# Two transformer blocks on one core: the first weights loaded in two halves, and the parameter rows moved behind them, in the lead-in of the kernel

## The reference, cut to what matters

```python
for i in range(DEPTH):
    h = rmsnorm(x, ln1_g[i]) @ w_in[i]
    (fq, fk, fv, ff, dq, dk, dv, c_q, c_kv, k_r) = jnp.split(h, split_points, axis=-1)
    o_fox = fox_group(fq, fk, fv, ff, fgate_b[i])
    o_diff = diff_group(dq, dk, dv, lam_q1[i], lam_k1[i], lam_q2[i], lam_k2[i], diff_norm_g[i], lam_init)
    o_mla = mla_group(c_q, c_kv, k_r, q_norm_g[i], w_uq[i], kv_norm_g[i], w_ukv[i], pos)
    x = x + jnp.concatenate([o_fox, o_diff, o_mla], axis=-1) @ w_o[i]
    up = causal_dwconv(rmsnorm(x, ln2_g[i]) @ w_up[i], conv_w[i], conv_b[i])
    g, u = up[..., :D_FF], up[..., D_FF:]
    x = x + (jax.nn.silu(g) * u) @ w_down[i]
x = rmsnorm(x, final_g)
...
```

## Time and profile before

| | |
|---|---|
| time, median of 3 runs | 1857.57 us (1857.36 to 1857.59) |
| span of the profiled execution, first to last instruction | 1854.4 us |
| the time outside that span (launch and end), by the median | 3.2 us |
| PE busy | 1454.0 us (78%) |
| DVE busy | 799.2 us (43%) |
| ACT busy | 571.2 us (31%) |
| moved by DMA | 563.14 MB, mean 304 GB/s |

### The profile page before, as it was taken

The page is one execution under the profiler, slowest core; times in us unless marked ns, Lnnn a source line. Parts: engine busy times, 40 slices in busy tenths (PEclk is TensorE's granted clock), DMA queues, the critical chain, the costliest instruction groups (busy, mean ns, idle before and its releaser), DMA issues.

```text
span 1854.4 us, 24842 instructions
## 1 busy us (share of the span) xinstructions
PE 1454.0 (78%) x10541; PEld 1069.3 (58%) x10541; DVE 799.2 (43%) x1246; ACT 571.2 (31%) x898; POOL 62.2 (3%) x56
## 2 busy tenths in 40 slices
PE   8999999999999999985555445579999555555546
PEld 7999999989999898861212112149886121111212
DVE  5767777776777799830101001019973010000101
ACT  4655555465554585321000000028532100000001
POOL 1010000010000000100000000002010000000000
PEclk9999999999999999998777778789999877777868
DMA  9426555534655385799999999997479999999997
GB/s 325 145 70 226 191 174 173 171 104 154 199 182 182 110 271 161 294 372 430 429 430 430 430 429 429 430 394 245 153 293 369 430 429 429 430 430 429 430 429 315
DMA packets 165492, 563.14 MB, mean 304 GB/s; under 512 B 12600, under 2 KB 116534, under 8 KB 137606
## 3 DMA queue, kind: packets, MB, share of 16 engines
q1 hardware_dynamic: 155318, 551.49, 76.2%
q10 hardware_dynamic: 10064, 10.06, 1.8%
HBM read 558.05 MB, written 1.05 MB: 301 GB/s over the span
## 4 chain that ended last, share of the span: by engine, by line
PE 54%; issue 23%; DMA 17%; DVE 3%; ACT 2%; POOL 1%; SPq 0%; POOLq 0%; PEldq 0%; ACTq 0%; DVEq 0%
PE psum L2682 6%; PE psum L2721 5%; PE psum L2976 5%; PE psum L2659 5%; PE psum L2661 5%; PE psum L2660 5%; DMA ring<-in_w_down 5%; DMA ring<-in_w_up 3%; DMA arena<-in_w_gate 3%; PE psum L2711 3%; PE psum L2831 2%; PE psum L2958 2%; PE psum L2576 2%; DMA arena<-in_w_down 2%; DMA arena<-in_w_up 2%
## 5 line engine op out<-in xcount | busy, mean ns | idle before, releaser
L2976 PE MATMUL psum<-ring,arena 128*32 128x512 f32 (+1 forms) x1600 | 280.6, 691 | 198.4 <-DMA ring<-in_w_down 77.8
L2976 PE MATMUL psum<-arena 128*32 128x512 f32 x1024 | 207.6, 702 | 149.5 <-DMA ring<-in_w_up 40.3
L2976 PEld LDWEIGHTS psum<-ring,arena 128*32 128x32 f32 x1600 | 70.7, 128 | 346.0 <-issue 343.4
L907 DVE TENSOR_TENSOR W<-ring,W 128x2048 fp32r<-128x2048 f32 (+1 forms) x92 | 206.3, 2243 | 85.1 <-ACT W L888 84.5
L2274 DVE TENSOR_TENSOR arena<-arena,psum 128x512 f32<-128x512 f32 x16 | 11.0, 690 | 452.7 <-PE psum L2976 452.7
L2659 PE MATMUL psum<-XT,W 128*128 128x256 f32 x704 | 199.4, 283 | 0.0
L2661 PE MATMUL psum<-XT,W 128*128 128x256 f32 x704 | 199.1, 283 | 0.0
L2660 PE MATMUL psum<-XT,W 128*128 128x256 f32 x704 | 199.0, 283 | 0.0
L888 ACT ACTIVATE W<-ring 128x2048 fp32r<-128x2048 f32 (+1 forms) x92 | 172.3, 1872 | 78.7 <-PE psum L2661 42.5
L2976 PEld LDWEIGHTS psum<-arena 128*32 128x32 f32 x1024 | 50.5, 127 | 251.4 <-issue 251.4
L2660 PEld LDWEIGHTS psum<-XT,W 128*128 128x128 f32 x704 | 134.9, 192 | 0.9
(11 more groups left out here) (341 smaller groups left out, 2619.0 us busy)
## 6 DMA issues: line engine op xcount, KB each, us to landing
ring<-in_w_down SPq DMA_DIRECT2D x36, 2048.0 KB, 30.0
ring<-in_w_up SPq DMA_DIRECT2D x32, 2048.0 KB, 31.2
ring<-in_w_up SPq DMA_DIRECT2D x58, 1024.0 KB, 5.1
ring<-in_w_gate SPq DMA_DIRECT2D x28, 2048.0 KB, 33.5
ring<-in_w_in SPq DMA_DIRECT2D x54, 1024.0 KB, 7.6
arena<-in_w_up SPq DMA_DIRECT2D x24, 2048.0 KB, 32.9
arena<-in_w_down SPq DMA_DIRECT2D x20, 2048.0 KB, 29.9
arena<-in_w_gate SPq DMA_DIRECT2D x20, 2048.0 KB, 29.8
```

What stands on the lines that cost most here:

```text
L907: nc.vector.tensor_tensor(W2[split_pair(v)][:, c], slot(v % SLOTS_1)[:, c], W1[split_pair(v)][:, c].bitcast(F32), ALU.subtract).then_inc(r ...
L2976: last = nc.tensor.matmul(psum[CAP * e:CAP * (e + 1), b, 0:cols.stop - cols.start], src[:, 4 * half + k, CAP * e:CAP * (e + 1)], tiles[e][ ...
```

## The change: what it does

1. SP loads block 0 in two halves, `k` 0 and 1, then `k` 2 and 3; the six parameter rows of SP come only after block 1 and piece 2.
2. ACT makes the first parts of `k` 2 and 3 first, then rounds the first half of block 0, the second half, and makes the first parts of `k` 4 to 7. Only then does it issue its seven parameter rows and `wf`, and goes on to block 1.
3. DVE makes the second parts of `k` 0 to 3 before the difference of block 0; its four copies of turned parameter rows come after the copy of the norm's root.
4. PE starts `latents(0)` when the first half is rounded, without the transposes of parameter rows; in it the products with `XT2` go ahead of those with `W2`. The four transposes come after the two of the norm's root, into bank 7 in place of 6, and the wait for the copies moves from block 2 to block 3.

```diff
@@ sync
-                        sp.dma_start(raw_latents(i), columns(w["w_in"], lay, c0, n)[:, 4 * i:4 * i + 4]).then_inc(slot_loaded[i], 16)
                         if lay == i == 0:
+                            src = columns(w["w_in"], lay, c0, n)
+                            sp.dma_start(raw_latents(i)[:, 0:2], src[:, 0:2]).then_inc(s_lamr, 16)
+                            sp.dma_start(raw_latents(i)[:, 2:4], src[:, 2:4]).then_inc(slot_loaded[i], 16)
+                        else:
+                            sp.dma_start(raw_latents(i), columns(w["w_in"], lay, c0, n)[:, 4 * i:4 * i + 4]).then_inc(slot_loaded[i], 16)
+                    else:
+                        load(u % SLOTS_1, columns(w["w_in"], lay, c0, n), n)
+                        if lay == 0 and i == 2:
                             sp.wait_ge(s_zero, 5)
                             for dst, src in parameter_rows()[1::2]:
                                 sp.dma_start(dst, src).then_inc(s_rows, 16)
-                    else:
-                        load(u % SLOTS_1, columns(w["w_in"], lay, c0, n), n)
@@ scalar
-            for dst, src in parameter_rows()[0::2]:
-                act.dma_start(dst, src).then_inc(s_rows, 16)
-            act.dma_start(wf, w["w_in"][0].rearrange("(k p) n -> p k n", p=P)[:, :, 768:772]).then_inc(wu_loaded, 16)
             act.wait_ge(s_small, SMALL)
...
-                    split_round(act, past, 0)
-                if lay == 0:
                     act.wait_ge(s_gain, 18)
-                turn_split_act(act, past, 0, 0, par[:, C_LN1:C_LN1 + 8] if lay else first_gain_cols, FIRST_BANK[lay], ENTRY_BY_DVE[lay])
-                if lay == 0:
+                    turn_split_act(act, past, 0, 0, first_gain_cols, FIRST_BANK[lay], ENTRY_BY_DVE[lay] + tuple(range(4, KD)))
+                    act.wait_ge(s_lamr, 16)
+                    nc.scalar.activation(latent_weights(W1[0])[:, 0:2], raw_latents(0)[:, 0:2], ACT.Copy).then_inc(s_lame, 1)
+                    act.wait_ge(slot_loaded[0], 16)
+                    act.sem_clear(slot_loaded[0])
+                    nc.scalar.activation(latent_weights(W1[0])[:, 2:4], raw_latents(0)[:, 2:4], ACT.Copy).then_inc(rounded, 1)
+                    turn_split_act(act, past, 0, 0, first_gain_cols, FIRST_BANK[lay], tuple(range(4)))
+                    for dst, src in parameter_rows()[0::2]:
+                        act.dma_start(dst, src).then_inc(s_rows, 16)
+                    act.dma_start(wf, w["w_in"][0].rearrange("(k p) n -> p k n", p=P)[:, :, 768:772]).then_inc(wu_loaded, 16)
                     split_round(act, past, 1)
@@ vector
-                    if k == 2 and lay == 0:
+                    if k == 4 and lay == 0:
+                        dve.wait_ge(s_lame, 1)
                         split_rest(dve, past, 0)
-                        parameters()
...
                 nc.vector.tensor_copy(root_cols, psum[:, 1, 0:S]).then_inc(root_table, 1)
+                if lay == 0:
+                    parameters()
@@ tensor
-            pe.wait_ge(s_rows, ROWS)
-            for l in range(DEPTH):
-                for i in range(2):
-                    nc.tensor.transpose(psum[:, 6, P * (2 * l + i):P * (2 * l + i + 1)], rows[:, l, i, :], ident).then_inc(s_rowsT, 1)
...
-                    pe.wait_ge(rounded, past(rounded) + SPLIT_AT[i] + 1)
+                    if lay == i == 0:
+                        pe.wait_ge(s_lame, 1)
+                    else:
+                        pe.wait_ge(rounded, past(rounded) + SPLIT_AT[i] + 1)
                     for k in range(4 * i, 4 * i + 4):
+                        if lay == i == 0 and k == 2:
+                            pe.wait_ge(rounded, past(rounded) + SPLIT_AT[i] + 1)
...
+                    if lay or i:
+                        with_rests()
                     for k in range(4 * i, 4 * i + 4):
                         pe.wait_ge(xt_rest, past(xt_rest) + k + 1)
...
+                    if lay == i == 0:
+                        with_rests()
...
                 last.then_inc(root_table, 1)
+                if lay == 0:
+                    pe.wait_ge(s_rows, ROWS)
+                    for l in range(DEPTH):
+                        for i in range(2):
+                            nc.tensor.transpose(psum[:, 7, P * (2 * l + i):P * (2 * l + i + 1)], rows[:, l, i, :], ident).then_inc(s_rowsT, 1)
```

More of the change, by code:

```diff
@@ L534, in build @@
         s_lamd = sem("lambda_dots_differences_and_ones")
-        s_lame = sem("setup_exps")
+        s_lame = sem("first_half_rounded_then_setup_exps")
         slot_loaded = [sem(f"slot_loaded{i}") for i in range(SLOTS)]
@@ L546, in quad_loaded @@
             return slot_loaded[ring_slot(lay, 2 + q % QUAD_SEMS)]
-        s_lamr = sem("lambda_rows")
+        s_lamr = sem("first_half_loaded_then_lambda_rows")
         wu_loaded = sem("mla_weights_loaded")
@@ L683, in before @@
             return past
-        SMALL, ROWS, LAMBDA_ROWS = 16 * 2, 16 * 13, 16 * 5
+        SMALL, ROWS, LAMBDA_ROWS = 16 * 2, 16 * 13, 16 + 16 * 5
         def parameter_rows():
@@ L1176, in _ @@
                     act.dma_start(wf, w["w_in"][lay].rearrange("(k p) n -> p k n", p=P)[:, :, 768:772]).then_inc(wu_loaded, 16)
+                    turn_split_act(act, past, 0, 0, par[:, C_LN1:C_LN1 + 8], FIRST_BANK[lay], ENTRY_BY_DVE[lay])
                 else:
-                    split_round(act, past, 0)
-                if lay == 0:
                     act.wait_ge(s_gain, 18)
-                turn_split_act(act, past, 0, 0, par[:, C_LN1:C_LN1 + 8] if lay else first_gain_cols, FIRST_BANK[lay], ENTRY_BY_DVE[lay])
-                if lay == 0:
+                    turn_split_act(act, past, 0, 0, first_gain_cols, FIRST_BANK[lay], ENTRY_BY_DVE[lay] + tuple(range(4, KD)))
[8 more added lines that the diff above has]
+                    act.dma_start(wf, w["w_in"][0].rearrange("(k p) n -> p k n", p=P)[:, :, 768:772]).then_inc(wu_loaded, 16)
                     split_round(act, past, 1)
@@ L1603, in parameters @@
                         dve.wait_ge(s_rowsT, 2 * DEPTH)
-                        nc.vector.tensor_copy(par_all[:, l, P * i:P * i + P], psum[:, 6, P * (2 * l + i):P * (2 * l + i + 1)]).then_inc(s_par, 1)
+                        nc.vector.tensor_copy(par_all[:, l, P * i:P * i + P], psum[:, 7, P * (2 * l + i):P * (2 * l + i + 1)]).then_inc(s_par, 1)
                 dve.wait_ge(s_par, 2 * DEPTH)
@@ L1621, in lambdas @@
                     if l == 0:
-                        dve.wait_ge(s_lame, 1)
+                        dve.wait_ge(s_lame, 2)
                     nc.vector.tensor_tensor(par_all[:, l, C_NLAM:C_NLAM + 1], lame[:, 2 * l + 1:2 * l + 2],
@@ L1648, in lower_bounds @@
                 step(nc.vector.tensor_tensor(lb_t[:, 12:16], low[1], lb_t[:, 0:4], ALU.subtract))
-                dve.wait_ge(s_lame, 2)
+                dve.wait_ge(s_lame, 3)
                 step(nc.vector.tensor_tensor(lb_t[:, 16:20], lb_t[:, 8:12], lb_t[:, 12:16], ALU.add))
@@ L2393, in latents, with with_rests @@
                                              start=(k == 0), stop=False)
-                    split_ready(i)
-                    for k in range(4 * i, 4 * i + 4):
-                        for t in range(TT):
-                            nc.tensor.matmul(banks[t], XT1[:, k, t * P:(t + 1) * P], w2[:, k % 4, 0:LATENTS],
-                                             start=False, stop=False)
+                    def with_rests():
+                        split_ready(i)
+                        for k in range(4 * i, 4 * i + 4):
+                            for t in range(TT):
+                                nc.tensor.matmul(banks[t], XT1[:, k, t * P:(t + 1) * P], w2[:, k % 4, 0:LATENTS],
+                                                 start=False, stop=False)
+                    if lay or i:
+                        with_rests()
                     for k in range(4 * i, 4 * i + 4):
@@ L2420, in block @@
                         split_ready(i)
-                        if lay == 0 and i == 2:
+                        if lay == 0 and i == 3:
                             pe.wait_ge(s_par, 2 * DEPTH)
```

## The result

The changed kernel takes 1864.89 us (median of 5 runs, 1863.72 to 1866.15) beside 1857.57 us of the kernel before (5 runs, 1856.0 to 1858.9). The ratio is 1.0041, with a 95% interval of 1.0031 to 1.0052: 7.3 us slower, and the interval leaves out 1. The forecast was 1865.3 us.

What follows compares the result with a forecast made beforehand. PE bounds the first 18 of 40 slices, then DMA; lead-in shifts of PE reach the end one for one. 5.4 + 1.9 + 0.4 = 7.7 us takes 1857.57 to 1865.3 us, range 1862.7 to 1868.6 (chance 0.62).

Steps and rivals of the forecast that it cites:

- First products at 10.2: Lead-in, PE: first products start at 10.2 us, behind its last transpose, in place of 12.2.
- the clock gives most of that back: First 24 products: with the clock still rising at 14.9 us they end at 16.5, 1.0 us earlier; otherwise 14.4.
- `wf` issued at 13.6: ACT's eight issues begin at 10.2 us; `wf`, the last, follows 3.37 us later, at 13.6.
- Travel 8.4: `wf` takes 8.4 us from issue to landing, at 22.0 us; 5.8 and 9.4 kept as bounds.
- Narrow products +5.4: PE waits for `wf`: narrow products start at 22.9 us, not 17.54, +5.4 us (+2.8 to +6.4).
- Clock 1.9: Behind PE's idle wait, 3.8 us of work at half speed lose 1.9 us (0 to 4.2).
- Transposes 0.4: Four parameter-row transposes, turned later, add 0.4 us to PE; their DVE copies cost nothing.
- 3.2 us outside the span: Whole kernel: the median lies 3.2 us above the span, so span 1862.1 us gives median 1865.3.
- as meant: Rival: `wf` lands in time, by 15.6 us, 2.0 us after issue; 1857.0 us, at best 1854.9; chance 0.16.
- Short wait: Rival: ACT's queue gets its turn beside SP's backlog, `wf` lands after 5.8 us; 1860.8 to 1862.7 us; chance 0.19.
- Longer: Rival: `wf` finds SP's queue deeper, or the clock comes back late twice; over 1868.6 us; chance 0.03.
- The halves don't come sooner: Rival: SP delivers block 0's first half only at 9.9 us, first products start at 11; forecast time unchanged.

Runs made afterwards that it cites:

- gate first: Changed kernel with `wf` issued early, and its rounding on ACT and difference on DVE put ahead of block 1's: 1856.09 us, ratio 0.9992.
- 68 idle products: Changed kernel with 68 idle products in front of PE's wait for the rounded gate columns: 1870.58 us, ratio 1.0076.
- keeping PE busy: Changed kernel with 34 idle products in front of PE's wait for the rounded gate columns: 1862.82 us, ratio 1.0031.
- `wf` early: Changed kernel with `wf` issued where it stood before, behind ACT's table load, the seven parameter rows staying late: 1856.23 us, ratio 0.9996.

## Why the prediction was right, point by point

- **What bounds it.** "Every microsecond by which PE's products move" goes to the end: shown. PE lagged 7.40 us at block 2 and 7.42 at 407 us. For the changed kernel and all ten variants, the shift of block 2 in the profile and the difference of the medians agree within 1.3 us, from -2.1 and -0.9 (gate first) to +12.5 and +13.4 (68 idle products).
- **First products at 10.2:** 9.89. ACT's two first parts took 0.84 us, as estimated, but started at 8.21. The gain of the change was there, and hidden. The step "the clock gives most of that back", with a rise still at 14.9, was wrong: the clock rose within the first eight products, so the 24 ended at 14.45, near the lower of the two figures given (14.4 and 16.5). The whole 3.1 us went into a longer wait, and so this error did not touch the sum.
- **`wf` issued at 13.6:** 12.93. ACT's eight issues start at 9.84, and the last begins 3.09 us after the first, not 3.37.
- **Travel 8.4:** the reading was an upper bound, since the next issue of ACT at 13.42 only shows that `wf` had landed by then, and no packet of the queue moved after 12.6. It measured 8.6 to the activation (the chain's piece is 8.61), 8.3 and 9.3 in the two runs that issued it elsewhere. The choice of "the same transfer beside the same load" over the 256-packet row was the right one.
- **Narrow products +5.4:** +4.7 (22.23 against 17.54). The 0.7 us over are those of the issue time; a travel 0.2 us longer and hand-overs 0.2 us shorter than allowed (21.56 to 22.23, 0.7 in place of 0.9) cancel. This is the term that was over-priced.
- **Clock 1.9:** the granted clock was 0.50 for 4.87 us, and keeping PE busy gave back 2.3. Under-priced by 0.4 in this execution, over-priced by 0.6 in another of the same lead-in (1.3); both inside 0 to 4.2.
- **Transposes 0.4:** the six take 0.58 us (31.48 to 32.06) against 0.13 for two before, so 0.4. The copies of DVE at nothing: PE has no wait at blocks 2 or 3.
- **Sum 7.7 in the lead-in:** 7.4. The 0.7 us too much for `wf` and the 0.4 too little for the clock offset each other, and of the agreement to 0.4 us that much is luck; in an execution with the cheaper clock the lead-in's lag was 6.35.
- **3.2 us outside the span:** wrong. It is 1.8. The prediction took the difference between one profiled execution and the median of others for a part outside the span. This did not matter, since the sum was added to the median. It does explain why the spans differ by 9.0 us and the medians by 7.3: the profile of the kernel before is of an execution some 1.4 us faster than its median, one of the two that kept the clock at 400 us (1.2 us).
- **Range of the forecast:** its lower end, 1862.7, doesn't follow from the reason given. The sum without any of the clock's price is 1863.4 us.

Of the rivals, "as meant" fails by its own criterion: `wf` would have had to travel 2.0 us, less still with the 24 products ending at 14.45, and even with SP's queue held back it takes 2.8. "Short wait" is excluded at 1024 packets, and its 5.8 us is nearly what 128 packets took (5.6). "Longer" did not occur: the travel was 8.6 us, 0.2 over what was taken. The round-robin rule of the Trainium skill ("DMA: Bandwidth & Descriptors", "Queues, rings and completion order") does describe the middle of the travel: from 17 to 21 us q10 moved 1035 packets beside 1174 of q1. It doesn't cover the start: `wf` was issued at 12.93 and its packets moved from about 17 us on, and 128 packets behind the backlog took 5.6 us where 1024 without it took 2.8. "The halves don't come sooner" didn't occur: half of block 0 was being rounded at 8.94, where before the whole began at 9.96.

**What stays open.** Whether the 4 us at the start of the travel are spent in making the descriptors, in a queue ahead of the engines or in memory was not tried. Why the clock falls at 410 us in one kernel's profiled execution and not in another's, behind the same 2.3 us of idle time, is not known, nor why it comes back sooner in one execution of the same lead-in than in another; each kernel has one profile. The changed kernel and the one with the gate first were filled at that place, and a similar fall near 804 us in the kernel with `wf` early was left as it is. Of the 1.6 us that the early `wf` gains at block 2, 0.9 shows in the median, and neither is certain to differ from nothing.

## What to carry to other kernels

When a group of small transfers is moved later, look at the first use of each one: PE was ready for what the last of the group brings 1.5 us after its new issue (14.45 and 12.93), while the seven before it had time until the norm's root. A small transfer that is issued into another queue's backlog should be given the travel time that it showed beside the same load, however few bytes it has, and where it can't be issued early, a wait on it in the queue of the bulk loads can take it out of the backlog (here 8.6 us became 2.8, at no visible cost). Price a new idle stretch of PE with what the lower clock costs behind it: here the later start lost 4.7 us and the clock another 1.3 to 2.3, by execution.

## What the runs showed of the hardware that I had not expected

- **Travel hardly depends on when the transfer is issued, as long as there is a backlog.** 8.3, 8.6 and 9.3 us to the activation for issues at 10.41, 12.93 and 9.62 us, and 2.8 us at 12.99 without one. 2 KB beside the backlog took 5.6, twice what 16 KB took without it. In the four runs beside the backlog some 4 us pass before the transfer's packets move.
- **An idle stretch of 2.33 us can be followed by a low clock, or not.** In the kernel with `wf` early, at the same place in the program:

```profile
401.30:404.50 3.20, 3.20 (x17) 3.20 (x17) 1.88 (x4) 3.20 (x13) 0.00 (x0) 0.50 0.83 259
```

  Here PE has 17 instructions in 3.20 us at 0.50, where the kernel before has 31 in 3.60 us at 1.00. In the changed kernel the lag behind the kernel before grows by 1.2 us from 407 us (7.42) to 647 us (8.60), with this fall between. The clock fell at this place in eight of the ten profiled executions without a fill, at some 1.2 us each. It also fell behind the 2.54 us of waiting in the old kernel with `wf` late, after the work had begun again.
- **An idle product of 128 x 128 in fp32 takes 0.22 us**, twice a transpose of the same size (0.11): the profile lists 68 instructions for 34 products.
